# Out-projection by Strassen's seven half-size products, and one RG-LRU tile's short taps moved off VectorE

## What is computed

```
u = rms_norm(x) @ w_in                      # 1024 -> 5 groups of 1024
xr = causal_dwconv(xr, w of width 4)        # the "short taps"
hr = rg_lru(xr)                             # gates, then a scan over time
y_r = hr * silu(gr)
v  = causal_dwconv(cv_v * sigmoid(cv_g), w of width 31)
v  = silu(layer_norm(v))
y_c = (v @ cv_w_pw2 + cv_b_pw2) * silu(gc)
y  = concat([y_r, y_c]) @ w_out             # 2048 -> 1024, on 1056 tokens
out = x + rms_norm(y, post_g)
```

## Time and the profile before

| what | us |
|---|---|
| median of 3 runs | 828.98 (828.12 to 829.11) |
| profiled execution, its own time | 828.99 |
| its span | 827.0 |
| TensorE busy | 804.9 |
| VectorE busy | 571.2 |
| ScalarE busy | 371.6 |
| GpSimd busy | 259.0 |

### The profile page before, as it was taken

How to read it: one execution, slowest core, us unless ns; L and a number is a source line. 1 busy time by engine, 2 the same in 40 slices (tenths; PEclk the granted TensorE clock), 3 DMA queues, 4 the chain that set the end, 5 groups by cost and what they waited for, 6 DMA issues and landing times. The chain is left out here.

```text
span 827.0 us, 12188 instructions
## 1 busy us (share of the span) xinstructions
PE 804.9 (97%) x4964; PEld 783.6 (95%) x4964; DVE 571.2 (69%) x510; ACT 371.6 (45%) x568; POOL 259.0 (31%) x156
## 2 busy tenths in 40 slices
PE   6999999999999999999999989899999999999996
PEld 4999999999999999999999978899999999999996
DVE  6589999999989959959959987962519322212225
ACT  6622482482482482482482458932517212211221
POOL 5224445446456455555464613010110000000000
PEclk8999999999999999999999999999999999999999
DMA  8311212202202302302302300423191111011047
GB/s 276 80 52 52 70 33 78 78 26 77 85 17 77 99 4 77 102 0 77 103 0 77 103 25 1 157 80 100 55 326 52 52 52 52 29 47 51 25 143 276
DMA packets 78737, 65.44 MB, mean 79 GB/s; under 512 B 2587, under 2 KB 71835, under 8 KB 78706
## 3 DMA queue, kind: packets, MB, share of 16 engines
q1 hardware_dynamic: 77776, 63.91, 23.9%
q0 software_dynamic: 928, 1.12, 0.6%
q10 hardware_dynamic: 2, 0.00, 0.0%
HBM read 51.77 MB, written 13.25 MB: 79 GB/s over the span
## 5 line engine op out<-in xcount | busy, mean ns | idle before, releaser
L731 PE MATMUL ps<-act_hi,w_hi 128*128 128x352 f32 (+5 forms) x1320 | 433.8, 329 | 1.1 <-DVE act_lo L1558 0.6
L733 PE MATMUL ps<-act_hi,w_lo 128*128 128x352 f32 (+5 forms) x1320 | 427.8, 324 | 0.0
L732 PE MATMUL ps<-act_lo,w_hi 128*128 128x352 f32 (+2 forms) x1128 | 366.0, 324 | 0.0
L1618 DVE SCALAR_TENSOR_TENSOR ps<-cv_in,par_cv,ps 128x1086 f32<-128x1086 f32 x232 | 313.8, 1353 | 7.8
L731 PEld LDWEIGHTS ps<-act_hi,w_hi 128*128 128x128 f32 x1320 | 248.5, 188 | 7.9 <-issue 6.8
L733 PEld LDWEIGHTS ps<-act_hi,w_lo 128*128 128x128 f32 x1320 | 248.6, 188 | 0.1
L732 PEld LDWEIGHTS ps<-act_lo,w_hi 128*128 128x128 f32 x1128 | 212.6, 188 | 0.4 <-issue 0.3
L586 POOL TENSOR_TENSOR w_lo<-wstage,w_hi 128x1024 fp32r<-128x1024 f32 x40 | 98.5, 2478 | 84.4 <-ACT w_hi L1064 84.2
L1064 ACT ACTIVATE w_hi<-wstage 128x1024 fp32r<-128x1024 f32 x63 | 65.7, 1054 | 101.4 <-PE ps L733 89.6
L1538 DVE TENSOR_TENSOR w_lo<-wstage,w_hi 128x1024 fp32r<-128x1024 f32 x24 | 30.3, 1262 | 60.5 <-ACT w_hi L1064 60.5
L731 PE MATMUL ps<-act_lo,w_hi 128*128 128x416 f32 (+2 forms) x192 | 63.4, 330 | 0.0
(11 more groups left out here) (193 smaller groups left out, 803.9 us busy)
## 6 DMA issues: line engine op xcount, KB each, us to landing
wstage<-in_w_in SPq DMA_DIRECT2D x40, 512.0 KB, 3.8
wstage<-in_w_out SPq DMA_DIRECT2D x16, 512.0 KB, 3.7
silu_spill<-silu_gc SPq DMA_DIRECT2D x8, 528.0 KB, 2.7
yr_spill<-y_rg SPq DMA_DIRECT2D x8, 528.0 KB, 2.7
silu_l<-silu_spill SPq DMA_DIRECT2D x8, 528.0 KB, 3.9
yr<-yr_spill SPq DMA_DIRECT2D x1, 4224.0 KB, 13.1
wstage<-in_cv_w_pw SPq DMA_DIRECT2D x8, 512.0 KB, 4.6
x_in<-in_x_prompt SPq DMA_DIRECT2D x7, 512.0 KB, 6.2
```

Source lines behind the costliest of these rows:

```text
L731: pe.matmul(out, wh, xh, start=start, stop=False)
L732: pe.matmul(out, wh, xl, start=False, stop=False)
L733: return pe.matmul(out, wl, xh, start=False, stop=stop)
L1618: STT(out=acc, in0=src, scalar=w, in1=acc, op0=ALU.mult, op1=ALU.add).then_inc(taps, 1)
```

## The change

**The product.** The 2048 x 1024 weight and the activations are cut in halves: output tiles 0 to 3 and 4 to 7, the yr half and the yc half of the input, tokens 0 to 527 and 528 to 1055 (`TH` = 528). Seven products replace eight. Each product p has four steps (one per output tile ei), 28 steps in all; a step is 8 k x 2 chunks of 264 columns x 3 matmuls = 48, so 1344 matmuls. Products 0, 1, 3, 4 and 6 use a sum or difference of two weight blocks, made by GpSimd (`weight_sum`, 20 of them, 128 x 1024). Products 1, 2, 3, 5 and 6 use a sum or difference of two activation half rows, also by GpSimd (`operand_sum`, 40 of them, 128 x 528). ScalarE and VectorE split every operand anew (`operand_high`, `operand_low`, 56 each, 128 x 528; `out_high`, `out_low`, 28 each, 128 x 1024). The results are gathered in `c_out` by ScalarE copies and VectorE additions; the finished half rows are squared, scaled, turned and placed by ScalarE.

```
+PRODUCTS = [((0, 0), ALU.add, (0, 1)), ((0, 1), ALU.subtract, (1, 1)), ((1, 1), None, None),
+            ((0, 0), ALU.add, (1, 1)), ((1, 0), ALU.add, (1, 1)), ((0, 0), None, None),
+            ((1, 0), ALU.subtract, (0, 0))]
```

**Loads (SP).** 48 blocks of 512 KB instead of 16, in five slots (`OUT_STAGE`), each waiting for the slot's last reader. Block 4 waits for the state outputs. The residual rows of the first group of tokens are loaded in the middle of the block loads:

```
+                if i < N_STAGE:
+                    if i < 2:
+                        sp.wait_ge(late_los, LATE_PW + 7 + i)
+                    elif i < 4:
+                        sp.wait_ge(pw, 6)
+                    else:
+                        sp.wait_ge(st_out, 16 * 6)
...
+            for i in range(len(BLOCKS)):
+                if BLOCKS[i][0] == 5 * HT + 1 and BLOCKS[i][1] == 0:
+                    sp.wait_ge(b_low, 6 * KT)
+                    load_residual(0)
+                load_out(i)
```

**GpSimd.** `weight_sum(0)`, `weight_sum(1)`, the six state DMAs, then in each step s the next weight sum and two operand sums for the following product:

```
+            for s in range(STEPS):
+                if s >= 2:
+                    weight_sum(s)
+                for k in (2 * (s % HT), 2 * (s % HT) + 1):
+                    operand_sum(s // HT + 1, k)
```

**VectorE and ScalarE, per step** (the first cut to its core; `add_product` is one addition of 528 columns from PSUM in products 1, 2, 3 and 6, two in 4 and 5):

```
+            out_low(0)
+            for k in range(KT):
+                operand_low(0, k)
             pw_out(KT - 1)
...
+            out_low(1)
+            next_operand_low(-1)
+            for s in range(PAIRED):
+                got = ps[:, 2 * (s % 2):2 * (s % 2) + 2, 0:TC]
+                dve.wait_ge(oproj, s + 1)
+                add_product(s, got)
+                out_low(s + 2)
+                if s >= FINAL:
+                    add_squares(s, got)
+                next_operand_low(s)
...
+            for s in range(PAIRED):
+                p, ei = divmod(s, HT)
+                out_high(s + 2)
+                act.wait_ge(oproj, s + 1)
...
+                    A(got, two(c_half(e, h)), ACT.Square).then_inc(o_sq, 1)
+                    act.wait_ge(o_sq, f + 1)
+                    A(c_half(e, h), c_half(e, h), ACT.Copy, scale=par[:, e, P_PG:P_PG + 1]).then_inc(o_scaled, 1)
+                next_operand_high(s)
...
+                if s >= FINAL:
+                    place_half(f, e, h)
```

**TensorE.** In step s it waits for `late_los` of that step and for its PSUM banks; after k = 5 of a step it turns the half row of the step before (`turn_half`, five transposes, waits for `o_scaled`) from step 13 on:

```
+                pe.wait_ge(late_los, LATE_OUT + s + 1)
+                bank_free(s)
...
+                    if k == 5 and s > FINAL:
+                        turn_half(s - 1)
```

**Seventh tile's short taps.** `RTAPS_AT[6]` is None. ScalarE forms the three products of the taps (into `cv_in` and a new `rg_tmp`), GpSimd adds them to `rg_x`, three additions of 128 x 1080 ahead of `rg_low`; ScalarE's copy of the gr weights is moved ahead of the read of x:

```
+                if last:
+                    for k in range(1, RW):
+                        pool.wait_ge(rproducts, k)
+                        if k > 1:
+                            pool.wait_ge(rtaps, 3 * c + k - 1)
+                        TT(rg_x[:, :], rg_x[:, :], r_product(k), ALU.add).then_inc(rtaps, 1)
                 rg_low(c)
```

More of the change, by code:

```diff
@@ L979, in earlier_sums @@
[L979 to L994, removed]
@@ new lines, in turn_half @@
+            def turn_half(s):
+                p, f = s // HT, s - FINAL
+                e, h = s % HT + (p in (4, 6)) * HT, p // 5
+                pe.wait_ge(o_scaled, f + 1)
+                if f == 0:
+                    pe.wait_ge(yc, KT)
+                else:
+                    pe.wait_ge(o_placed, f)
+                row = c_half(e, h)
+                for i in range(4):
+                    pe.transpose(ps[:, 4, i * P:(i + 1) * P], row[:, i * P:(i + 1) * P], ident[:, :])
+                pe.transpose(ps[0:16, 5, 0:P], row[:, 4 * P:TH], ident[:, :]).then_inc(o_turned, 1)
@@ new lines, in turn_tiles, with sums @@
+            def turn_tiles(j, src, bank):
+                for i, (c0, rows) in enumerate(OUT_TILES[j]):
+                    mm = pe.transpose(ps[0:rows, bank, i * P:(i + 1) * P], src[:, i * P:i * P + rows], ident[:, :])
+                mm.then_inc(o_turned, 1)
+            def sums(j, src, fst, last):
+                for i, (c0, rows) in enumerate(OUT_TILES[j]):
+                    mm = pe.matmul(ps[0:rows, 7, i:i + 1], src[:, i * P:i * P + rows], mean_w[:, 0:1],
+                                   start=fst and i == 0, stop=last, skip_group_check=True)
+                if last:
+                    mm.then_inc(ss_done, 1)
@@ new lines, in square_scale @@
+            def square_scale(e, c0, n, out, done, i):
+                act.wait_ge(c_added, additions(PAIRED - 1) + i)
+                row = c_half(e, 1)[:, c0:c0 + n]
+                A(out, row, ACT.Square).then_inc(done, 1)
+                if done is o_sq:
+                    act.wait_ge(o_sq, PAIRED - FINAL + (1 if i == 1 else 2))
+                else:
+                    act.wait_ge(last_sqd, 1)
+                A(row, row, ACT.Copy, scale=par[:, e, P_PG:P_PG + 1]).then_inc(o_scaled, 1)
@@ new lines, in add_squares, with rstd @@
+            def add_squares(s, got):
+                f, h = s - FINAL, s // HT // 5
+                dve.wait_ge(o_sq, f + 1)
+                if f % KT == 0:
+                    dve.tensor_copy(two(ssq[h]), got).then_inc(o_ssq, 1)
+                else:
+                    dve.wait_ge(o_ssq, f)
+                    TT(two(ssq[h]), two(ssq[h]), got, ALU.add).then_inc(o_ssq, 1)
+            def rstd(j):
+                n, whole = TILE_BASE[j], sum(rows == P for c0, rows in OUT_TILES[j])
+                dve.wait_ge(ss_root, n + len(OUT_TILES[j]))
+                dve.reciprocal(rs_o[:, 1, n:n + whole], rs_o[:, 0, n:n + whole]).then_inc(ss_rs, 1)
+                if j < 2:
+                    dve.reciprocal(rs_o[0:16, 1, n + whole:n + whole + 1],
+                                   rs_o[0:16, 0, n + whole:n + whole + 1]).then_inc(ss_rs, 1)
@@ L1891, in _ @@
+            add_chunk(KT - 1, *CHUNK_B, 3, 4)
+            y_out(1, 1)
+            y_out(1, 2)
+            dve.wait_ge(o_turned, half + 4)
+            dve.wait_ge(last_sqd, 2)
+            dve.tensor_copy(c_half(KT - 1, 1)[:, 0:2 * P], ps[:, 5, 0:2 * P]).then_inc(o_placed, 1)
             rstd(2)
+            dve.wait_ge(ss_rs, 5)
+            dve.wait_ge(o_placed, half + 4)
+            dve.wait_ge(xr_loaded[2], 16 * 2)
             for i in range(2):
-                for a in (0, 2):
-                    y_part(2, i, a, a + 2)
+                for a in range(2):
+                    y_out(2, i, a, a + 1)
```

632 lines of the change are left out of this document (377 added, 255 removed).

## The result

The changed kernel takes 832.84 us (median of 5 runs, 831.51 to 834.58), the kernel before 829.1 (828.12 to 829.19) on the same chip: ratio 1.0049, interval 1.0034 to 1.0064. It is slower by 3.7 us, where 832.7 was predicted. Its profiled execution took 833.25, with a span of 830.4 against 827.0.

A forecast was written before the change was run, and what follows sets the result against it. TensorE, busy 97% of the span, was taken as the bound. Stage +6.2 (203.5 against 197.3), tail +2.2 and taps -4.7 make +3.7 on 828.99: 832.7 us, own range 827.5 to 837, 8 in 10 within 818 to 840.

The forecast's parts named there:

- unobstructed stage: Out-projection without waits: 163.3 us of matmuls, 8.6 of transposes, 1.4 of single-column sums, together 173.3 us.
- loss up to step 8: Start of the out-projection: step 8 at 688.5 instead of 669.1, a loss of 19.4 us, bounds 7 and 23.
- loss in product 4: Steps of product 4: 7.2 us against TensorE's 6.38, a loss of 2.5 us, bounds 0 and 5.
- loss by the residual loads: Step 20: weight block late behind five residual loads, TensorE stands 7.3 us, slower clock 1: loss 8.3 us.
- tail, more than before: After the last matmul: VectorE's remaining work and the last store take 9.4 us instead of 7.2, 2.2 more.
- ahead of the stage (taps): Seventh tile's taps off VectorE: 3.8 us wait for csum gone, mean products 0.9 shorter, gain 4.7 us.
- rival E: Out-projection: the seven products do not get cheaper, weight loads bounding at 264 columns: 854 us, chance 0.03.
- The exclusion: Out-projection: GpSimd and two-SBUF-input VectorE instructions run one after the other, whole: 7.2 to 7.5 us per step against 5.83.
- Rival A: Out-projection: exclusion only partial, GpSimd's sums run beside VectorE, start costs 7, product 4 nothing: 817.8 us, chance 0.18.
- The start itself: First steps of the out-projection: TensorE starts at 627 instead of 622.5, step 1 at 633.8.
- Rival B: Step 20: exclusion holds, but the weight block of step 21 is not late: 824.4 us, chance 0.14.
- Rival D: Seventh tile: the moved taps come too late for the gates, so the stop only moves there: 837 us, chance 0.06.

The follow-up runs named there:

- experiment 3: Changed kernel with the five residual loads placed ahead of the weight blocks of step 25 instead of step 21: 821.0 us, ratio 0.9896.
- experiment 4: Changed kernel with VectorE's subtractions of steps 1 to 8 and products 1 and 2 reading their second input from PSUM: 827.15 us, ratio 0.9965.
- experiment 7: Changed kernel with experiment 3's edit, operand sums of products 1 and 2 on VectorE, and state stores ahead of the first weight sum: 816.2 us.
- experiment 1: Changed kernel with the seventh tile's three short taps back on VectorE, seven products kept: 838.34 us, ratio 1.01.

## Why the prediction was right

The mechanisms that the prediction names are confirmed by the runs. That the total came within 0.2 us is luck: its terms were off by up to 4 us, +6.9 in all one way and -7.2 the other, and cancelled.

| term | predicted | measured |
|---|---|---|
| unobstructed stage | 173.3 | 176.1 |
| loss up to step 8 | 19.4 | 15.4 |
| loss in product 4 | 2.5 | 1.1 |
| loss by the residual loads | 8.3 | 12.1 |
| rest of the stage | 0 | 0.3 |
| tail, more than before | 2.2 | 1.7 |
| ahead of the stage (taps) | -4.7 | -6.0 |

**The products.** Steps 8 to 12 of the changed kernel start at 678.91, 684.79, 690.67, 696.55 and 702.43: 5.88 us for 48 matmuls of 264 columns, 0.1225 us each, 164.6 for 1344 instead of 163.3. The single-column sums were counted at half their cost: there are 13 calls ahead of the last matmul's end, but each is two instructions of 0.11 us. The rows have ten for the five calls of one group:

```profile
775.04 1.08 PE L1158 MATMUL ps<-mean_w,yr 128*128 128x1 f32 x10
```

In experiment 3, where TensorE does not stop in front of it, the step with them takes 7.53 us and one without 6.42. So the 13 sums cost 2.9 us and not 1.4, and with the predicted 8.6 for transposes the unobstructed stage is 176.1. The weight load does not bound at 264 columns, so rival E is out. The Trainium skill (TensorE: Matmul & The Clock Gate, "Wait — 56ns, not 53.3ns?") has N / 2.4 GHz plus 2.5 ns, as an estimate 112.5 ns; the trace differs from it at 264 as it did at 256, and the measurement decides.

**The exclusion** was read rightly from four stretched instructions, and experiment 4 shows it. The Trainium skill (SBUF — State Buffer, "SBUF: two separate sides") has the same rule: GpSimd and a VectorE instruction with two SBUF inputs share a pair of ports as a lock for the whole instruction, and the loser waits. By that rule, the trace agrees: 4.44 us for two `operand_low` beside GpSimd, 1.31 without a second SBUF input. To the last 0.2 us it does not, as follows, and the measurement decides. The size of the exclusion was too large by the assumption "one after the other, whole". Alone, a step's instructions take 2.39 + 2.39 on GpSimd and 1.22 + 1.31 on VectorE, 7.3 us; the steps came every 6.63. Some 0.7 us a step overlap, about 0.2 for each of VectorE's three instructions. The rows before had this already: L586 at 485.78 and VectorE's instruction that ends at 486.46 overlap by 0.68 us, and L586 is only 0.47 longer than 2.41, which the prediction rounded to "0.5 of waiting". From step 1 to step 8 the prediction had 54.7 us, the trace has 49.0. Rival A, engines that do not hold each other up, is out; and with the exclusion out of the way in experiment 4 the loss up to step 8 is still 9.5, where the prediction had 7.

**The start itself** was sized too small. Step 1 begins 13.4 us after the end of `pw`, not 11.3. Two things: the first weight sum starts 1.9 us ahead of that end, not 3.1, since `pw` ends 6.0 us earlier than in the trace before and that sum begins only 4.8 earlier than predicted (614.58 for 619.4); and "The half clock after the stops at the start costs nothing, because there the next step waits for VectorE anyway" is wrong. Steps 1 and 3 begin without a wait for VectorE, and the slower clock costs 2.0 and 1.6 us in front of them.

**Product 4.** The transposes of successive steps begin at 712.72, 719.14, 725.56, 731.98 and 738.39, so a step with them takes 6.42 us, and TensorE waits for nobody there. In step 18, the last of this stretch, it waits 0.66 us (745.84), for ScalarE's scale, which had waited for VectorE's additions. From step 8 to step 19 the changed kernel takes 69.0 us (678.91 to 747.91), against 11 x 5.88 + 6 x 0.54 = 67.9: a loss of 1.1, inside the bounds of 0 and 5.

**The residual loads.** Place, chain and stop were as predicted; the size was 12.1 for 8.3, and the stop in it 10.1, outside the 6.5 to 8.5 given for it. The residual loads are let go 6.9 us after the end of step 18 (754.85 - 747.91), against 4.5 to 6.5. From there to the use of the block are 766.46 - 754.85 = 11.6 us, against 10.6: the queues move 298 GB/s rather than 313, and SP needs 3.58 us to issue the five loads before the block. The clock behind the stop cost 2.0, not 1. Rival B, no late block, did not come; experiment 3 is what it would have been.

**The rest of the stage**, 0.3 us, is the difference of the sum of these terms to 205.0. One more wait of 0.2 us (808.71) is in it.

**The tail** was 0.5 us shorter than its sum.

**The taps.** The cause was right, the price of the clock too low. csum is done 6.1 us earlier (479.14 for 485.27), but it is no longer what counts: the mean product starts at 481.12, when TensorE gets there, 4.2 us earlier than before. That is the wait of 3.8; 0.2 more is no work of the change, since this trace runs 0.2 ahead from 440 us on. From that start until VectorE may subtract are 2.0 us instead of 3.6, at the clock of 1.00 instead of 0.50: 1.6 us, where the prediction had 0.9. Rival D, gates late, is out: `rg_low` ends at 466.25 and the gates start at 466.88, without a new wait. The three additions on GpSimd and the copies on ScalarE lie beside the 23 long taps, which keep their pace: 31.89 us for the 23 from 443.36 on, 1.387 each, as before.

## What to carry to other kernels

Work that is taken off the bounding engine is paid for by the engines and queues that prepare its operands: here 20 us of matmuls were removed, and 28.6 us were lost in three places; of the 16.6 us that came back (832.84 - 816.2) 12 came back by the order in one queue. Before GpSimd is given work beside a busy VectorE, count both engines' instructions with two SBUF inputs as one queue, and give VectorE's an input in PSUM, or one of the engines fewer instructions, where the sum passes the step. When an edit to a late event gains nothing, look for a second cause of the same lateness before it is called harmless; and keep bulk loads, and the event that they wait for, behind the next blocks that a tight loop needs.

## What the runs showed of the hardware

A GpSimd and a VectorE instruction, each with two inputs in SBUF, hold each other up, but by some 0.2 us less than the whole length of the other (7.3 us of work in a step of 6.63); with one VectorE input in PSUM both run at the lengths that they have alone. With TensorE's waits of 3.44, 5.56 and 9.95 us in the changed kernel the granted clock fell to 1.2 GHz, which cost another 1.6, 2.0 and 2.0 us. In the waits of 5.56 and 9.95 us it had fallen before TensorE resumed; with the wait of 3.44 us the fall came 0.7 us after it:

```profile
639.87 0.28 PE L889 MATMUL ps<-act_hi,w_hi 128*128 128x264 f32 x1
639.99 0.36 PE L890 MATMUL ps<-act_hi,w_hi 128*128 128x264 f32 x1
640.15 0.42 PE L891 MATMUL ps<-act_hi,w_lo 128*128 128x264 f32 x1
```

Matmuls go from 0.12 us apart to 0.22. Behind the waits of 0.5 us in steps 5 to 7, of 1.04 us in experiment 7, of 1.77 us in experiment 4 and of 3.02 us in experiment 1 the clock stayed at 1.00. So the price of a wait is not its length alone: 3.44 us cost 5.0, 9.95 cost 12, and 1.77 cost 1.8.
